# Value transposes of an HGRN2 head issued behind its diagonal products, in one place of the TensorE stream

## The chip, the cores and the metric

One core of one Trainium2 chip runs the whole program. The metric is the device time of one execution in microseconds; of several runs the median is given.

## The reference, cut to what matters

Two layers over 1024 prompt tokens and 8x4 sample tokens, width 1024, all float32. Layer 0 is a gated short convolution, layer 1 the HGRN2 recurrence with 8 heads of 128x128 state. The change touches layer 1 alone. There each head h needs four projections (q, f, i, z) of all 1056 tokens and the chunked recurrence:

```python
proj = h @ w_in
q, fpre, inp, z = jnp.split(proj, 4, axis=-1)
q = silu(q) * HEAD_DK ** -0.5 ; vv = inp
log_f = maximum(logaddexp(log(lb), log1p(-lb) + log_sigmoid(fpre)), LOG_F_FLOOR)
k = -expm1(log_f)
# per head: S_t = diag(f_t) S_{t-1} + k_t^T v_t ,  o_t = q_t S_t
o, S = hgrn2_chunked(q, k, vv, log_f, s0)
o = rms_norm(o, g_onorm) ; y = (o * silu(z)) @ w_out
```

The prompt starts from a zero state, the sample rows from `state_hgrn`, one state per batch entry.

## The kernel before, in words

**Layout.** Activations lie feature by token: the projection of one head is a tile of 128 features by 1056 tokens, computed as three groups of 352 tokens, each 24 matmuls (8 slices of the input width, three high/low products of split fp32r operands; line 565). Four projections of a head are thus 12 groups. While the projections of head j run, the recurrence of head j-1 is done in places between the groups: `iteration(j, last)` (line 887) calls `rec(j-1, s, last)` after group s, s = 0 to 11, on TensorE, on VectorE (line 1873 on) and on ScalarE (line 1277). There is no planner; the order of each engine's queue is this hand-written one, and engines meet at semaphores. `Events` objects (PR for TensorE, VR for VectorE, AR for ScalarE) number the signals of a head in the order in which they are issued, so a wait names a signal and the count follows. The last head (h = 7) has no projections beside it; there the places are filled with parts of the output projection (`first_parts`, `part`) and with idle transposes (`keep_pace`, line 928) (lines 921 to 948).

**The places that matter here.** Place s=0: nine transposes turn the output of the head before (lines 794, 795). Place s=1, TensorE: eight transposes of the values `r_vr` into banks 5 and 6, one of the three-fold stacked sample values into bank 7 (lines 809, 810), signal `vt`. ScalarE then copies bank 7 to `v_stk` (line 1296, signal `vh`) and banks 5, 6 to `r_vt` (line 1298, signal `vt`), and writes the high half of the earlier head's output (`turn_hi`, line 1273). VectorE at s=1 multiplies the keys and queries by their gates (line 1903, 2112 columns, signal `kq`), then subtracts in `v_stk` (line 1907, `vl`), copies the sample values (line 1909, `vs`), and writes the low half of the earlier head's output (`turn_lo`, line 1871). Place s=3, TensorE: after waiting for `vs`, 16 products of 64x64 on the diagonal (line 816; 32 records in the trace, since each product is recorded twice) and one of 32x32 for the samples (line 818, two records), signal `dg`. VectorE at s=3 waits for `dg`, then line 1915 (`u2`), two predicated copies (line 1918, `am`), one small one (line 1922, `as`), then twice a whole-width multiply and a small one (lines 1928, 1931, `w4`), line 1936, 1937, and at last the stacked keys into `k_stk` (line 1940, `k3c`), for which it first waits for GpSimd. Place s=5, TensorE: waits for `k3c`, transposes the stacked keys (line 822) and runs the products of level 8 (line 786).

**GpSimd** (`spread_v`, line 511): per head a memset of ones, after `kq` a memset of the score tile (line 519, signal `am_zero`), and after `vs` one multiply of 96x1024 elements that spreads the stacked sample values over the batch entries (line 521, signal `pool_rec`). It reads `v_stk`, which shares its memory with `k_stk`; hence the wait before line 1940.

**Weights.** Each projection's weights are loaded by the SP queue, split by ScalarE (line 984, high half) and VectorE (line 1426, low half, `split_lo`) into two slots, one projection ahead. In the last head the same two lines split the rows of the output weights; `first_parts(k)` waits for `split_lo` of row k.

Of the kernel before, what the change touches and what calls it, by code (L numbers as in the profile page):

```python
# [22 lines left out]
F32 = mybir.dt.float32  # L23
F32R = mybir.dt.float32r
U8 = mybir.dt.uint8
ALU = mybir.AluOpType
ACT = mybir.ActivationFunctionType
AX = mybir.AxisListType

P = 128  # L30
# [5 lines left out]
NSAMP = NB * NS  # L36
# [3 lines left out]
CK = NP // P  # L40
# [44 lines left out]
def build(nc, x_prompt, x_sample, state_conv, state_hgrn, norm_pre, w_in, conv_w, lb_logits, onorm,  # L85
          w_out, norm_post, y_prompt, y_sample, conv_p, conv_s, hgrn_p, hgrn_s):
    ctx = ExitStack()
    with ctx:
# [3 lines left out]
        def sem(name):  # L92
            return ctx.enter_context(nc.semaphore(name))
# [35 lines left out]
        ident = sb("ident", [P, P])  # L129
# [66 lines left out]
        r_vt = pl.take((CK + 1) * P)  # L196
# [9 lines left out]
        STK = 3 * NSAMP  # L206
# [26 lines left out]
        def o_part(i, half):  # L233
# [53 lines left out]
        S_SUM = Events(sem("sample_sum_dve"), ["y0", "y1"])  # L287
        V_Y = Events(sem("out2_sum"), ["y0", "y1"])
        q_sig, z_sig = sem("q_sig"), sem("z_sig")
        PR = Events(sem("rec_pe"), ["vt", "dg", "kst", "L8", "L16", "us", "os", "L32", "L64",  # L290
                                    "kt", "u", "o0", "o1"])
        VR = Events(sem("rec_dve"), ["lb", "v3", "qc", "k", "fa", "f", "tt", "g4", "g3", "ri", "i3", "i2", "i1", "kq",
                                     "vl", "vs", "u2", "am", "as", "w4", "u4", "qb", "k3c", "kl", "w8", "c8", "u8", "w16", "c16", "u16", "w32", "c32", "u32", "ss",
                                     "sn0", "snew", "w64", "c64", "u64"]
                    + [f"s{c}" for c in range(CK)] + ["r0", "r1", "rs", "on0", "on1", "ons"])
        AR = Events(sem("rec_act"), ["gc", "vh", "vt", "kts", "os", "sqs", "kt", "sq0", "sq1", "sd"])
# [233 lines left out]
        def _(pe):  # L530
# [239 lines left out]
            def tokens(c, n=P):  # L770
                return slice(c * P, c * P + n)
# [25 lines left out]
            def rec(h, s, last):  # L797

                if s == 0:
                    if last is not None:  # L800
                        turn_output(last)
                elif s == 1:
                    for c in range(NCH):
                        pe.wait_ge(bank_free[c], emptied(bank_use(NW2) + 2 + 4 * h))
                    if last is not None:
                        pe.wait_ge(o_rdy, last + 1)
                    pe.wait_ge(VR.sem, VR.at(h, "v3"))
                    for c in range(CK):
                        nc.tensor.transpose(bank[5 + c // 4][:, tokens(c % 4)], r_vr[:, tokens(c)], ident[:, :])
                    nc.tensor.transpose(bank[7][0:STK, 128:256], r_vt[:, CK * P:CK * P + STK], ident[:, :]).then_inc(PR.now("vt"), 1)  # L810
                elif s == 3:

                    pe.wait_ge(VR.sem, VR.at(h, "vs"))
                    for i in range(2 * CK):
                        at, rows = i * HP, slice(i % 2 * HP, (i % 2 + 1) * HP)
                        nc.tensor.matmul(bank[3 + i // CK][rows, i % CK * HP:(i % CK + 1) * HP], r_K[:, at:at + HP],  # L816
                                         r_Q[:, at:at + HP], start=True, stop=True)
                    nc.tensor.matmul(bank[7][0:NSAMP, 0:NSAMP], r_K[:, NP:], r_Q[:, NP:], start=True,
                                     stop=True).then_inc(PR.now("dg"), 1)
                elif s == 5:  # L820
                    pe.wait_ge(VR.sem, VR.at(h, "k3c"))
                    nc.tensor.transpose(bank[7][0:STK, 0:P], k_stk[:, 0:STK], ident[:, :]).then_inc(PR.now("kst"), 1)
# [153 lines left out]
        def _(act):  # L976
# [293 lines left out]
            def turn_hi(h):  # L1270

                act.wait_ge(o_rdy, h + 1)
                A(reg_b[:, bass.ds(h * 2 * T, T)], r_o, ACT.Copy).then_inc(o_hi, 1)
# [3 lines left out]
            def rec(h, s, last):  # L1277
# [10 lines left out]
                elif s == 1:  # L1288

                    if last is None:  # L1290
                        act.wait_ge(V_TR.sem, V_TR.at(TT - 1, "lo"))
                    else:
                        act.wait_ge(sp_out, h * 16)
                    act.dma_start(states, state_hgrn[0, :, bass.ds(h, 1)].rearrange("b h k v -> k (b h) v")).then_inc(s0_in, 16)
                    act.wait_ge(PR.sem, PR.at(h, "vt"))
                    A(v_stk[0:STK, :], bank[7][0:STK, P:2 * P], ACT.Copy).then_inc(AR.now("vh"), 1)
                    for half in range(2):
                        ins = A(r_vt[:, half * 512:(half + 1) * 512], bank[5 + half][:, :], ACT.Copy)
                    ins.then_inc(AR.now("vt"), 1)
                    if last is not None:  # L1300
                        turn_hi(last)
                elif s == 5:
                    act.wait_ge(PR.sem, PR.at(h, "kst"))
                    act.wait_ge(pool_rec, h + 1)
                    A(kv_stk[0:STK, CK * P:], bank[7][0:STK, 0:P], ACT.Copy).then_inc(AR.now("kts"), 1)
                elif s == 6:
                    act.wait_ge(PR.sem, PR.at(h, "os"))
                    A(r_os[:, :], bank[7][:, 0:P], ACT.Copy).then_inc(AR.now("os"), 1)
                    act.wait_ge(AR.sem, AR.at(h, "os"))
                    A(bank[7][:, P:2 * P], r_os[:, :], ACT.Square,  # L1310
                      accum_out=small[:, CK:CK + 1]).then_inc(AR.now("sqs"), 1)
                elif s == 7:
                    act.wait_ge(VR.sem, VR.at(h, "snew"))
                    act.dma_start(hgrn_s[0, :, bass.ds(h, 1)].rearrange("b h k v -> k (b h) v"), states).then_inc(s0_out, 16)
                elif s == 8:
                    act.wait_ge(PR.sem, PR.at(h, "kt"))
                    for half in range(2):
                        ins = A(r_kt[:, half * 512:(half + 1) * 512], bank[5 + half][:, :], ACT.Copy)
                    ins.then_inc(AR.now("kt"), 1)
                elif s == 10:  # L1320
                    act.wait_ge(PR.sem, PR.at(h, "o1"))
                    for half in range(2):
                        A(r_sq[:, half * 512:(half + 1) * 512], bank[3 + half][:, :], ACT.Square).then_inc(AR.now(f"sq{half}"), 1)
                    act.wait_ge(VR.sem, VR.at(h, "r1"))
                    A(small[:, 16:17 + CK], small[:, 0:CK + 1], ACT.Sqrt, bias=eps[:, :], scale=1.0 / P).then_inc(AR.now("sd"), 1)
                    act.wait_ge(VR.sem, VR.at(h, f"s{CK - 1}"))
                    act.dma_start(hgrn_p[0, 0, bass.ds(h, 1)].rearrange("h k v -> k (h v)"),
                                  r_s[:, (CK - 1) * P:]).then_inc(sp_out, 16)
# [90 lines left out]
        def _(dve):  # L1419
# [454 lines left out]
            def rec(h, s, last, final=False):  # L1874
# [23 lines left out]
                elif s == 1:  # L1898
# [2 lines left out]
                    dve.wait_ge(AR.sem, AR.at(h, "gc"))  # L1901
                    dve.wait_ge(pool_one, h + 1)
                    V.tensor_tensor(r_kq, r_kq, arena[:, 0:2 * T], ALU.mult).then_inc(VR.now("kq"), 1)
                    dve.wait_ge(PR.sem, PR.at(h, "vt"))
                    dve.wait_ge(AR.sem, AR.at(h, "vh"))
                    third = slice(2 * NSAMP, 3 * NSAMP)
                    V.tensor_tensor(v_stk[third, :], bank[7][third, P:2 * P], v_stk[third, :].bitcast(F32),
                                    ALU.subtract).then_inc(VR.now("vl"), 1)
                    V.tensor_copy(r_vt[0:NSAMP, CK * P:], bank[7][0:NSAMP, P:2 * P]).then_inc(VR.now("vs"), 1)
                    if last is not None and not final:  # L1910
                        turn_lo(last)
                elif s == 3:
# [4 lines left out]
                    for half in range(2):  # L1917
                        ins = V.copy_predicated(r_am[:, half * 512:(half + 1) * 512].rearrange("p (c t) -> p c t", c=4),
                                                mask8[:, :].unsqueeze(1).broadcast_to([P, 4, P]),
                                                bank[3 + half][:, :].rearrange("p (c t) -> p c t", c=4))  # L1920
                    ins.then_inc(VR.now("am"), 1)
                    V.copy_predicated(r_as[:, :], mask4[:, :], bank[7][0:NSAMP, 0:NSAMP]).then_inc(VR.now("as"), 1)
                    dve.wait_ge(VR.sem, VR.at(h, "u2"))

# [154 lines left out]
```

## Time and profile before

| | us |
|---|---|
| median of 3 runs | 1077.96 |
| lowest, highest | 1077.11, 1078.79 |
| the profiled execution, its own time | 1079.18 |
| its span, first to last instruction | 1077.5 |
| TensorE busy in the span | 1052.9 (98%) |
| VectorE busy | 724.4 (67%) |
| ScalarE busy | 384.8 (36%) |
| GpSimd busy | 38.6 (4%) |

The mean granted TensorE clock of the span is 0.995 of full speed. Seven heads (h = 0 to 6) run beside projections, about 62 us each, from about 500 to 935 us; the last head and the output projection follow. In the rows of a timeline the columns are: start and duration in us, engine, line, operation, output <- input by the program's names, partitions x elements, count of merged instructions, and in brackets the idle time just before and what ended it. DVE is VectorE, ACT ScalarE, POOL GpSimd, PE TensorE. A matmul's duration runs to its modelled end, so its successor starts before that; starts are what tells the pace.

### The profile page before, as it was taken

To read this page: it belongs to the slowest core of one execution; us is meant where nothing else is said; L and a number is where in the kernel's file an instruction comes from. 1 tells how busy PE (TensorE), PEld (TensorE's weight loads), DVE (VectorE), ACT (ScalarE), POOL (GpSimd) and SP (SyncE) were. 2 spreads that over 40 slices of the span, in tenths; PEclk is the share of its full clock that TensorE was granted. 3 is DMA by queue.
4 is the path that set the end of the run, shared out by engine and by line. 5 is a ranking of instruction groups with operands and counts; after the bars stand their busy time and mean duration, and the time that the engine had idled before them with its cause. 6 is when DMAs were issued, how large, how long until landed. Compare 5 with 4: busy or idle time off the path is not lost.

```text
span 1077.5 us, 20495 instructions
## 1 busy us (share of the span) xinstructions
PE 1052.9 (98%) x8043; PEld 987.8 (92%) x8043; DVE 724.4 (67%) x1294; ACT 384.8 (36%) x730; POOL 38.6 (4%) x53
## 2 busy tenths in 40 slices
PE   6999999999999999999999999999999999979997
PEld 5999999999999888789999999999999999967885
DVE  7798677677677645655658595775859577575146
ACT  7443333333334433443243242414233241533123
POOL 1000000000000000000101010010101010010000
PEclk9999999999999999999999999999999999989999
DMA  7102121121121352122212211211221121121143
GB/s 231 33 20 79 42 77 39 39 78 39 39 78 58 115 181 99 64 64 59 60 42 60 60 41 58 60 40 41 58 61 41 56 61 58 42 79 59 47 174 123
DMA packets 93317, 74.30 MB, mean 69 GB/s; under 512 B 2519, under 2 KB 85528, under 8 KB 93274
## 3 DMA queue, kind: packets, MB, share of 16 engines
q1 hardware_dynamic: 75482, 64.80, 19.2%
q10 hardware_dynamic: 17792, 8.91, 2.8%
q8 instruction: 29, 0.48, 0.2%
q14 instruction: 14, 0.11, 0.0%
HBM read 60.26 MB, written 13.44 MB: 68 GB/s over the span
## 4 chain that ended last, share of the span: by engine, by line
PE 89%; DVE 7%; DMA 2%; issue 1%; ACT 1%; SPq 0%; DVEq 0%; ACTq 0%
PE bank L565 34%; PE bank L613 23%; PE bank L712 17%; PE bank L585 2%; PE bank L786 2%; PE bank L859 1%; PE bank L866 1%; PE bank L780 1%; PE bank L868 1%; DMA wraw<-in_w_in 1%; PE bank L816 1%; DMA arena<-in_x_prompt 1%; PE bank L727 1%; PE bank L693 1%; PE bank L689 1%
## 5 line engine op out<-in xcount | busy, mean ns | idle before, releaser
L565 PE MATMUL bank<-reg_a,wsplit 128*128 128x352 f32 x2304 | 388.5, 326 | 0.6 <-ACT arena L1236 0.6
L565 PEld LDWEIGHTS bank<-reg_a,wsplit 128*128 128x128 f32 x2304 | 367.8, 188 | 4.0 <-issue 2.4
L613 PE MATMUL bank<-reg_a,wsplit 128*128 128x264 f32 x1344 | 165.5, 284 | 0.0
L613 PEld LDWEIGHTS bank<-reg_a,wsplit 128*128 128x128 f32 x1344 | 164.1, 188 | 0.0
L613 PE MATMUL bank<-reg_b,w_ring 128*128 128x264 f32 x1008 | 125.0, 284 | 1.0 <-ACT arena L1091 1.0
L613 PEld LDWEIGHTS bank<-reg_b,w_ring 128*128 128x128 f32 x1008 | 123.3, 188 | 1.3 <-DVE arena L1545 1.0
L712 PE MATMUL bank<-reg_a,reg_b 128*128 128x512 f32 x288 | 71.3, 402 | 0.9 <-DVE reg_a L1426 0.9
L712 PE MATMUL bank<-reg_b,reg_a 128*128 128x512 f32 x288 | 68.7, 395 | 0.0
L712 PEld LDWEIGHTS bank<-reg_a,reg_b 128*128 128x128 f32 x288 | 55.0, 192 | 14.3 <-DVE reg_a L1426 1.3
L712 PEld LDWEIGHTS bank<-reg_b,reg_a 128*128 128x128 f32 x288 | 53.9, 188 | 12.6
L1614 DVE TENSOR_TENSOR arena<-arena,bank 128x264 f32<-128x264 f32 x84 | 34.8, 427 | 33.6 <-PE bank L613 32.4
L1069 ACT ACTIVATE w_ring<-wraw 128x512 fp32r<-128x512 f32 x42 | 26.1, 631 | 68.8 <-PE bank L613 68.8
L1091 ACT ACTIVATE arena<-bank 128x264 f32<-128x264 f32 x84 | 31.9, 389 | 48.8 <-PE bank L613 44.1
L1426 DVE TENSOR_TENSOR wsplit<-wraw,wsplit 128x1024 fp32r<-128x1024 f32 x36 | 43.8, 1218 | 4.7 <-ACT wsplit L984 4.7
L1069 ACT ACTIVATE wsplit<-wraw 128x512 fp32r<-128x512 f32 x42 | 25.0, 627 | 57.4 <-DMA wraw<-in_w_in 44.1
L1811 DVE TENSOR_TENSOR arena<-arena,r_tt 128x512 f32<-128x512 f32 x32 | 22.1, 689 | 32.3 <-PE bank L786 20.1
L1236 ACT ACTIVATE arena<-bank 128x352 f32<-128x352 f32 x24 | 11.1, 462 | 90.7 <-PE bank L565 61.4
L1731 DVE TENSOR_TENSOR arena<-bank,arena 128x512 f32<-128x512 f32 x24 | 16.3, 686 | 39.3 <-ACT arena L1182 39.2
L1998 DVE SCALAR_TENSOR_TENSOR arena<-arena,bank 128x352 f32<-128x352 f32 x45 | 22.7, 516 | 21.2 <-ACT arena L1234 12.0
L1234 ACT ACTIVATE arena<-bank 128x352 f32<-128x352 f32 x21 | 9.7, 464 | 74.5 <-PE bank L565 74.5
L984 ACT ACTIVATE wsplit<-wraw 128x1024 fp32r<-128x1024 f32 x34 | 35.8, 1056 | 0.0
L517 POOL MEMSET arena<- 128x264 f32 x8 | 5.5, 688 | 831.4 <-DVE r_tt L1858 783.8
(260 smaller groups left out, 1481.9 us busy)
## 6 DMA issues: line engine op xcount, KB each, us to landing
wraw<-in_w_in SPq DMA_DIRECT2D x64, 512.0 KB, 4.0
arena<-in_x_prompt SPq DMA_DIRECT2D x16, 512.0 KB, 3.6
wraw<-in_w_out SPq DMA_DIRECT2D x16, 512.0 KB, 3.3
x_scratch<-arena SPq DMA_DIRECT2D x8, 512.0 KB, 2.6
arena<-in_state_hgrn ACTq DMA_DIRECT2D x8, 512.0 KB, 3.9
out<-arena ACTq DMA_DIRECT2D x8, 512.0 KB, 3.0
arena<-x_scratch SPq DMA_DIRECT2D x8, 512.0 KB, 3.2
out<-arena SPq DMA_DIRECT2D x7, 512.0 KB, 2.9
```

Source lines behind the costliest of these rows:

```text
L565: mm = nc.tensor.matmul(bank[b][:, 0:CH], w[wi][:, k, :], rhs[hi], start=(k == 0 and i == 0), stop=(k == KT - 1 and i == 2))
L585: mm = nc.tensor.matmul(bank[b][:, 0:QT], w[wi][:, k, :], src[hi][:, k % KH, cols], start=(k == 0 and i == 0), stop=(k == KT - 1 and i == 2))
L613: mm = nc.tensor.matmul(bank[banks[q]][:, 0:QT], w[wi][:, k, :], B_OP[name][hi][:, k, q * QT:(q + 1) * QT], start=(start and k == 0 and i ...
L712: mm = nc.tensor.matmul(bank[b][0:r, :], src[side][:, k, i * P:i * P + r], w[wi][:, half * HALF:(half + 1) * HALF], start=(start and side ...
L786: mm = nc.tensor.matmul(b[rows, i * HP // 2:(i + 1) * HP // 2].rearrange("p (b r) -> p b r", r=m), r_K[:, at:at + HP], rhs, start=True, st ...
L984: A(wsplit[:, s, 0] if dst is None else dst, wraw[:, s], ACT.Copy).then_inc(w_hi, 1)
L1069: A(w_block(name)[0], A_RAW[name], ACT.Copy).then_inc(W_HI.now(name), 1)
L1091: A(dst[:, q * QT:(q + 1) * QT], bank[banks[q]][:, 0:QT], ACT.Copy).then_inc(C_ACT.now(f"{what}{s}{q}"), 1)
L1426: V.tensor_tensor(d, wraw[:, s], h.bitcast(F32), ALU.subtract).then_inc(w_lo, 1)
L1614: V.tensor_tensor(dst[:, cols], src[:, cols], bank[banks[q]][:, 0:QT], ALU.add).then_inc(C_DVE.now(f"{what}{s}{q}"), 1)
L1811: V.tensor_tensor(qr, qr, tl.unsqueeze(2).broadcast_to([P, nb, m]), ALU.mult)
L1998: V.scalar_tensor_tensor(buf[:, cols], buf[:, cols], QSCALE if kind == "q" else 1.0, bank[c][:, 0:CH], ALU.mult, ALU.mult).then_inc(bank_f ...
```

## The change

At TensorE place s=1 no longer does anything. Place s=3 now holds, in this order: the waits that s=1 had (the three banks emptied, the earlier output read), a wait for `kq` in place of `vs`, the transpose of the stacked sample values, the diagonal products (signal `dg`), and the eight transposes of the values (signal `vt`). ScalarE's two copies move from s=1 to s=3, the first released by `dg`, the second by `vt`; VectorE's lines 1907 and 1909 move from between `kq` and `turn_lo` to between `am` and `as`. The lists of signals are reordered to match.

```diff
--- before.py
+++ after.py
@@ -287,10 +287,10 @@
         S_SUM = Events(sem("sample_sum_dve"), ["y0", "y1"])
         V_Y = Events(sem("out2_sum"), ["y0", "y1"])
         q_sig, z_sig = sem("q_sig"), sem("z_sig")
-        PR = Events(sem("rec_pe"), ["vt", "dg", "kst", "L8", "L16", "us", "os", "L32", "L64",
+        PR = Events(sem("rec_pe"), ["dg", "vt", "kst", "L8", "L16", "us", "os", "L32", "L64",
                                     "kt", "u", "o0", "o1"])
         VR = Events(sem("rec_dve"), ["lb", "v3", "qc", "k", "fa", "f", "tt", "g4", "g3", "ri", "i3", "i2", "i1", "kq",
-                                     "vl", "vs", "u2", "am", "as", "w4", "u4", "qb", "k3c", "kl", "w8", "c8", "u8", "w16", "c16", "u16", "w32", "c32", "u32", "ss",
+                                     "u2", "am", "vl", "vs", "as", "w4", "u4", "qb", "k3c", "kl", "w8", "c8", "u8", "w16", "c16", "u16", "w32", "c32", "u32", "ss",
                                      "sn0", "snew", "w64", "c64", "u64"]
                     + [f"s{c}" for c in range(CK)] + ["r0", "r1", "rs", "on0", "on1", "ons"])
         AR = Events(sem("rec_act"), ["gc", "vh", "vt", "kts", "os", "sqs", "kt", "sq0", "sq1", "sd"])
@@ -799,24 +799,23 @@
                 if s == 0:
                     if last is not None:
                         turn_output(last)
-                elif s == 1:
+                elif s == 3:
+
                     for c in range(NCH):
                         pe.wait_ge(bank_free[c], emptied(bank_use(NW2) + 2 + 4 * h))
                     if last is not None:
                         pe.wait_ge(o_rdy, last + 1)
-                    pe.wait_ge(VR.sem, VR.at(h, "v3"))
-                    for c in range(CK):
-                        nc.tensor.transpose(bank[5 + c // 4][:, tokens(c % 4)], r_vr[:, tokens(c)], ident[:, :])
-                    nc.tensor.transpose(bank[7][0:STK, 128:256], r_vt[:, CK * P:CK * P + STK], ident[:, :]).then_inc(PR.now("vt"), 1)
-                elif s == 3:
-
-                    pe.wait_ge(VR.sem, VR.at(h, "vs"))
+                    pe.wait_ge(VR.sem, VR.at(h, "kq"))
+                    nc.tensor.transpose(bank[7][0:STK, 128:256], r_vt[:, CK * P:CK * P + STK], ident[:, :])
                     for i in range(2 * CK):
                         at, rows = i * HP, slice(i % 2 * HP, (i % 2 + 1) * HP)
                         nc.tensor.matmul(bank[3 + i // CK][rows, i % CK * HP:(i % CK + 1) * HP], r_K[:, at:at + HP],
                                          r_Q[:, at:at + HP], start=True, stop=True)
                     nc.tensor.matmul(bank[7][0:NSAMP, 0:NSAMP], r_K[:, NP:], r_Q[:, NP:], start=True,
                                      stop=True).then_inc(PR.now("dg"), 1)
+                    for c in range(CK):
+                        mm = nc.tensor.transpose(bank[5 + c // 4][:, tokens(c % 4)], r_vr[:, tokens(c)], ident[:, :])
+                    mm.then_inc(PR.now("vt"), 1)
                 elif s == 5:
                     pe.wait_ge(VR.sem, VR.at(h, "k3c"))
                     nc.tensor.transpose(bank[7][0:STK, 0:P], k_stk[:, 0:STK], ident[:, :]).then_inc(PR.now("kst"), 1)
@@ -1292,13 +1291,15 @@
                     else:
                         act.wait_ge(sp_out, h * 16)
                     act.dma_start(states, state_hgrn[0, :, bass.ds(h, 1)].rearrange("b h k v -> k (b h) v")).then_inc(s0_in, 16)
+                    if last is not None:
+                        turn_hi(last)
+                elif s == 3:
+                    act.wait_ge(PR.sem, PR.at(h, "dg"))
+                    A(v_stk[0:STK, :], bank[7][0:STK, P:2 * P], ACT.Copy).then_inc(AR.now("vh"), 1)
                     act.wait_ge(PR.sem, PR.at(h, "vt"))
-                    A(v_stk[0:STK, :], bank[7][0:STK, P:2 * P], ACT.Copy).then_inc(AR.now("vh"), 1)
                     for half in range(2):
                         ins = A(r_vt[:, half * 512:(half + 1) * 512], bank[5 + half][:, :], ACT.Copy)
                     ins.then_inc(AR.now("vt"), 1)
-                    if last is not None:
-                        turn_hi(last)
                 elif s == 5:
                     act.wait_ge(PR.sem, PR.at(h, "kst"))
                     act.wait_ge(pool_rec, h + 1)
@@ -1901,12 +1902,6 @@
                     dve.wait_ge(AR.sem, AR.at(h, "gc"))
                     dve.wait_ge(pool_one, h + 1)
                     V.tensor_tensor(r_kq, r_kq, arena[:, 0:2 * T], ALU.mult).then_inc(VR.now("kq"), 1)
-                    dve.wait_ge(PR.sem, PR.at(h, "vt"))
-                    dve.wait_ge(AR.sem, AR.at(h, "vh"))
-                    third = slice(2 * NSAMP, 3 * NSAMP)
-                    V.tensor_tensor(v_stk[third, :], bank[7][third, P:2 * P], v_stk[third, :].bitcast(F32),
-                                    ALU.subtract).then_inc(VR.now("vl"), 1)
-                    V.tensor_copy(r_vt[0:NSAMP, CK * P:], bank[7][0:NSAMP, P:2 * P]).then_inc(VR.now("vs"), 1)
                     if last is not None and not final:
                         turn_lo(last)
                 elif s == 3:
@@ -1919,6 +1914,11 @@
                                                 mask8[:, :].unsqueeze(1).broadcast_to([P, 4, P]),
                                                 bank[3 + half][:, :].rearrange("p (c t) -> p c t", c=4))
                     ins.then_inc(VR.now("am"), 1)
+                    dve.wait_ge(AR.sem, AR.at(h, "vh"))
+                    third = slice(2 * NSAMP, 3 * NSAMP)
+                    V.tensor_tensor(v_stk[third, :], bank[7][third, P:2 * P], v_stk[third, :].bitcast(F32),
+                                    ALU.subtract).then_inc(VR.now("vl"), 1)
+                    V.tensor_copy(r_vt[0:NSAMP, CK * P:], bank[7][0:NSAMP, P:2 * P]).then_inc(VR.now("vs"), 1)
                     V.copy_predicated(r_as[:, :], mask4[:, :], bank[7][0:NSAMP, 0:NSAMP]).then_inc(VR.now("as"), 1)
                     dve.wait_ge(VR.sem, VR.at(h, "u2"))
 
```

## Rows read from the trace of the kernel before

**Rows 1.** The page: the engines' busy time, the chain that ended last.
```profile
PE 1052.9 (98%) x8043; PEld 987.8 (92%) x8043; DVE 724.4 (67%) x1294; ACT 384.8 (36%) x730; POOL 38.6 (4%) x53
...
PE 89%; DVE 7%; DMA 2%; issue 1%; ACT 1%; SPq 0%; DVEq 0%; ACTq 0%
```

**Rows 2.** Timeline of TensorE around place s=1 of head 3; the last row up to 700 us.
```profile
692.55 1.04 PE L809 MATMUL bank<-ident,arena 128*128 128x128 f32 x8
693.42 0.27 PE L810 MATMUL bank<-ident,arena 128*96 128x128 f32 x1
...
693.70 6.57 PE L565 MATMUL bank<-reg_a,wsplit 128*128 128x352 f32 x40
```

**Rows 3.** Timeline of TensorE around place s=3 of head 3.
```profile
701.06 0.32 PE L565 MATMUL bank<-reg_a,wsplit 128*128 128x352 f32 x1
...
701.31 1.15 PE L816 MATMUL bank<-arena 128*64 128x64 f32 x32
...
702.57 0.59 PE L565 MATMUL bank<-reg_a,wsplit 128*128 128x352 f32 x2
```

**Rows 4.** Timeline of TensorE at place s=5 of head 3.
```profile
710.37 0.27 PE L822 MATMUL bank<-ident,r_os 128*96 128x128 f32 x1
710.57 1.12 PE L786 MATMUL bank<-arena 128*64 128x32 f32 x32
```

**Rows 5.** Timeline of TensorE in the last head: the first transpose after level 32.
```profile
969.62 0.33 PE L928 MATMUL bank<-ident 128*128 128x128 f32 x1
```

**Rows 6.** Timeline of VectorE in head 3.
```profile
697.29 2.34 DVE L1903 TENSOR_TENSOR arena<-arena 128x2112 f32<-128x2112 f32 x1
...
700.29 1.26 DVE L1871 TENSOR_TENSOR reg_b<-arena,reg_b 128x1056 f32 x1
...
702.68 0.92 DVE L1915 TENSOR_TENSOR r_tt<-r_tt 128x264 f32<-128x264 f32 x1 [0.24 <-PE bank L818]
...
704.85 1.21 DVE L1928 TENSOR_TENSOR arena<-arena,r_tt 128x1024 f32<-128x1024 f32 x1
...
707.95 1.22 DVE L1426 TENSOR_TENSOR wsplit<-wraw,wsplit 128x1024 fp32r<-128x1024 f32 x1
```

**Rows 7.** Timelines: GpSimd's multiply in heads 0, 3 and 7; VectorE's line 1915 in heads 0 and 7.
```profile
514.32 1.90 POOL L521 TENSOR_TENSOR kv_stacked<-v_stacked,bmask 96x1024 fp32r<-96x1024 f32 x1
...
516.92 0.43 DVE L1915 TENSOR_TENSOR r_tt<-r_tt 128x264 f32<-128x264 f32 x1 [0.24 <-PE bank L818]
...
700.61 2.70 POOL L521 TENSOR_TENSOR kv_stacked<-v_stacked,bmask 96x1024 fp32r<-96x1024 f32 x1
...
946.70 2.66 POOL L521 TENSOR_TENSOR kv_stacked<-v_stacked,bmask 96x1024 fp32r<-96x1024 f32 x1
...
947.77 1.88 DVE L1915 TENSOR_TENSOR r_tt<-r_tt 128x264 f32<-128x264 f32 x1 [0.17 <-PE bank L818]
```

**Rows 8.** Timeline of ScalarE in head 3.
```profile
693.91 1.07 ACT L1298 ACTIVATE arena<-bank 128x512 f32<-128x512 f32 x2
...
706.73 0.47 ACT L1234 ACTIVATE arena<-bank 128x352 f32<-128x352 f32 x1 [4.85 <-PE bank L565]
```

**Rows 9.** Timeline of the last head, VectorE and TensorE.
```profile
943.36 2.36 DVE L1903 TENSOR_TENSOR arena<-arena 128x2112 f32<-128x2112 f32 x1
...
946.40 1.15 PE L816 MATMUL bank<-arena 128*64 128x64 f32 x32 [1.18 <-DVE arena L1909]
...
949.87 1.04 PE L928 MATMUL bank<-ident 128*128 128x128 f32 x8
...
955.26 4.21 PE L712 MATMUL bank<-wsplit,reg_b 128*128 128x512 f32 x9 [4.36 <-DVE wsplit L1426]
...
961.33 2.35 PE L712 MATMUL bank<-reg_a,reg_b 128*128 128x512 f32 x9
```

**Rows 10.** Table by stretch of the last head: us; PE, PEld, DVE, ACT, POOL busy; granted clock; DMA share; GB/s.
```profile
951.00:954.27 3.27, 0.00 (x0) 0.00 (x0) 3.23 (x8) 1.04 (x1) 0.00 (x0) 1.00 0.00 0
...
955.26:961.10 5.84, 5.84 (x38) 4.49 (x40) 1.36 (x2) 1.07 (x2) 0.00 (x0) 0.50 0.55 182
```

## The prediction

> **What bounds the kernel now.** The page comes first: TensorE is busy 98% of the span and carries 89% of the chain that ended last, VectorE only 7% [rows 1]. So in the stretch from about 500 to 935 us, where a head's recurrence lies between the projections of the next, work or waits off TensorE cost nothing until they make it late. The second view is TensorE's timeline in one such head: its groups of matmuls follow one another without an idle stretch, at 0.16 us a matmul ((6.57 - 0.33) / 39) [rows 2]. The third view is the last head, which has no projections to hide behind. There TensorE waits 1.18 us for line 1909 before the diagonal products, and 4.36 us for line 1426, which stands in VectorE's queue behind the whole of its place s=3 [rows 9]. So the change has two accounts: seven heads in which only TensorE's own time counts, and one in which VectorE's queue does.
>
> The profiled execution took 1079.18 us, 1.7 more than its span and 1.2 more than the median. The changes below are made against that execution and then put on the median. A difference of 0.2%, 2.2 us, is about what a measurement of this kernel can tell from no change.
>
> **The place taken away on TensorE.** Does a place cost anything beside its own instructions? At s=1 the rows say no: the first transpose starts at 692.55, the projection is back at its pace at 693.70, which without the place would have been 692.55 + 0.16. The place cost 0.99 us, and its nine transposes at 0.11 each are 0.98 ((693.42 - 692.55) / 8) [rows 2]. Nothing is left for the switch, and the transposes stay. Place s=3 does pay for switching: from 701.06 to the second projection matmul after it, 702.57 + 0.26, less two paces, is 1.45 us, of which the products are about 1.1 [rows 3].
>
> The new place, from rows of the same kinds: the stacked transpose follows a projection without loss and the products follow it after 0.20, as line 786 follows line 822 [rows 4]; the products to the small one's end, 702.57 - 701.31 = 1.26 with the 0.12 of the switch in it [rows 3]; then eight transposes. The first transpose behind level 32 in the last head shows how that switch goes: it lasts 0.33 where another lasts 0.27 [rows 5, 2], 0.06 more. So 0.06 + 7 x 0.11 = 0.83 to the eighth's start and, as after s=1, 0.28 less one pace to the projection's pace, 0.12. Sum 0.20 + 1.26 + 0.83 + 0.12 = 2.41 against 0.99 + 1.45 = 2.44. The small gap ahead of the products also shrinks by about 0.03. That makes 0.03 to 0.08 us a head; I take 0.06, seven times: **-0.4 us**. Bounds: nothing, or 0.1 a head, -0.7.
>
> The Trainium skill (TensorEngine Tiling (Array Packing), Key Properties) says that a change of tiling mode drains TensorE. The new order has as many changes of mode as the old, so by that rule, too, the removed place gives nothing back.
>
> **Waits of the seven heads.** The products now wait for `kq`, the end of line 1903 at 699.63, and TensorE reaches them 0.98 earlier, at 700.33, since s=1 is empty: 0.7 us of cover [rows 6, 3]. VectorE loses lines 1907 and 1909 here (from 699.63 to 700.29, 0.66 us), so `turn_lo` and the two evacuations behind it move up; none of them is late. ScalarE's copies come behind the products: about 1.4 us ending near 704, while it is idle until 706.73 less 0.98 [rows 8]. Cost nothing. No DMA is issued in the moved lines; SP's queue sees only a release of weight slots that shifts by under 1.5 us, with a whole projection of cover.
>
> **VectorE's place s=3, and GpSimd.** This is the term that can hurt. GpSimd's multiply of line 521 is released by `vs`. It takes 1.90 us in head 0, where VectorE ran beside it nothing with both inputs in SBUF [rows 7]. In head 3 it takes 2.70: line 1871 held VectorE until 701.55, and 701.55 + 1.76 is where the multiply ends, 703.31. Line 1915, started at 702.68, ends 0.29 after that, at 703.60, in 0.92 where it takes 0.43 alone [rows 6, 7]. In the last head it starts at 947.77 and ends 0.29 after the multiply, in 1.88 us. Of the eight heads only the first shows no hold; in the other seven the 0.29 is the same. So the two engines shut each other out, an instruction at a time. Now `vs` comes behind `am`, and the next thing VectorE does that reads SBUF twice is line 1928. It gets the multiply's 1.9 us in its way, less 0.14 of its own start that overlaps and less the small line 1922: about 1.7. If line 1928 wins instead, the multiply is late and line 1940 waits for it: the same sum.
>
> The Trainium skill (SBUF — State Buffer, Who interferes with whom) says that a VectorE instruction with two SBUF inputs contends with a GpSimd one that reads SBUF, and that the loser blocks fully. That speaks against this change, since line 1928 is of that form; by it alone the stall is certain, the trace shows it only for line 1915 and, the other way about, for the multiply.
>
> New chain in a middle head: the products start 0.98 - 0.20 earlier, so `dg` reaches VectorE at 702.68 - 0.78 = 701.90; line 1915 alone 0.43; `am` and `as` 1.25 (703.60 to 704.85); lines 1907 and 1909 0.66; lines 1928 to 1940 3.10 (704.85 to 707.95); stall 1.7. That is 709.0 for `k3c`, before 707.95 [rows 6]. TensorE asks for it at 710.37 less 0.06 [rows 4]: 1.3 us of cover are left of 2.4. Line 1426 then ends at 710.2, TensorE needs its weights at 711.6. **Cost nothing**, by a margin that is no longer large. The bounds of the stall: 0, or 2.7, the whole of the longest row; both still fit.
>
> **The last head.** TensorE no longer waits for line 1909 but for line 1903, which ends at 945.72: the products start at 945.76 + 0.20 instead of 946.40, `dg` comes 0.44 earlier [rows 9]. VectorE then needed 1.88 + 1.25 + 3.09 = 6.22 to line 1426 (953.99); now 0.43 + 1.25 + 0.66 + 3.09 + 1.7 = 7.13. Net 7.13 - 6.22 - 0.44 = **+0.5 us**, straight on the path, since TensorE waits for that line 1426 [rows 9] and its own chain runs on from there. Bounds: with no stall on line 1928, 5.43 - 6.22 - 0.44 = -1.2; with 2.7, +1.5. I take 1.7 because rows 7 show the hold in seven heads of eight. The transposes behind the products end near 948.2, ScalarE's 1.4 us of copies near 949.6 [rows 8]; `keep_pace`, which waits for them now, stood at 949.87 and moves to about 950.3 [rows 9].
>
> The wait of 4.36 us also lowers the clock: the granted clock is 1.0 to 954.27, TensorE having done nothing since 951, and 0.5, the 1.2 GHz level, to 961.10 [rows 10]. Nine matmuls there take 4.21 us, the same nine later 2.35 [rows 9]; with the places between, the low clock costs some 2.5 us. The new idle stretch is about 4.5 us, so I keep this cost. It can fall differently from run to run, by up to that 2.5.
>
> **Sum.** -0.4 + 0.5 = +0.1 us: 1079.3 for the profiled execution, 1078.1 on the median; a hundredth of a per cent, so no change. Chance 0.78.
>
> **Rival, faster (0.13).** Line 1928 is not shut out, or the multiply runs wholly beside lines that don't mind it. Then the last head gives -1.2, and its idle stretch shrinks from 4.4 to 2.7 us, so that the clock may not fall: -2.5 more. With -0.4 that is -1.6 to -4.1: 1073.9 to 1076.4. For it: only line 1915 has been seen waiting. Against: it waits to the same 0.29 each time, and line 1928 has the same two inputs in SBUF.
>
> **Rival, slower (0.09).** TensorE waits for `k3c` at place s=5 of the middle heads. The point from which it decides is 1.3 us beyond my 709.0. It would need VectorE shut out twice, once by the multiply for line 1928 and again for a later line, some 3.3 us in all. Then each head pays the excess; 0.5 us a head is 3.5 in seven, plus 2 in the last head: 1083. For it: cover halves. Against: the multiply is one instruction of 1.9 us, and VectorE and GpSimd one behind the other wholly are already in my sum.
>
> That the change does nothing at all is inside the first case.
>
> **How the numbers follow.** The forecast is 1078.1. Its own range is +-1.9 (the clock's 2.5 cut at either end, the stall's bounds). Reaching into the faster case: 1075.9 to 1080.0. Faster by over 0.2%: 0.13; within: 0.78; slower: 0.09.
>
> **What the changed profile would show.** No transposes of line 809's kind between the second and third group of a head, and the place of the products some 2.4 us long, with no idle time before line 822. Line 1915 at 0.43 us in every head. Line 1928's first instance 2.9 instead of 1.2 us, or the multiply longer than 3 us. In the last head `dg` about 0.4 earlier and line 1426, with TensorE behind it, about 0.5 later against the products of the head before. An idle stretch ahead of line 822 in the middle heads, a first line 1928 of 1.2 us beside a multiply of 1.9, or a last head without the half clock would prove me wrong.

## The result, and the profile after

The changed kernel takes 1081.88 us, median of 7 runs (1080.05 to 1083.33), the kernel before 1077.11 beside it (7 runs, 1076.38 to 1079.38): ratio 1.004, interval 1.0028 to 1.0052. It is slower by 4.8 us in the medians (3.0 to 5.6 by the interval), where no change was forecast, and outside the range. The profiled execution took 1081.48 us, its span is 1079.8.

The page of the changed kernel, the lines that answer to [rows 1]:

```profile
PE 1051.5 (97%) x8043; PEld 985.0 (91%) x8043; DVE 734.0 (68%) x1294; ACT 386.5 (36%) x730; POOL 42.4 (4%) x53
...
PE 80%; DVE 11%; issue 3%; ACT 3%; DMA 2%; ACTq 0%; SPq 0%; DVEq 0%
```

TensorE does the same work in the same busy time, but the chain that ended last has moved off it: 80% where it was 89%, VectorE 11% where it was 7%. Something in the middle heads now waits for VectorE. The view of one line, L565 of the changed kernel, says what:

```profile
its engine sat idle before it (us, times) until:
  issue: 7.6, 14
  DVE wsplit L1427: 3.7, 7
  ACT arena L1235: 0.6, 1
```

Seven times, once a head, the projections wait for the VectorE half of the weight split (line 1427, line 1426 before): 0.2 us in head 0, 0.56 to 0.62 us in each of heads 1 to 6. The kernel before has no such entry. Its `issue` entry is 2.4, 8; the 5.2 us more here are the same six stops, seen from the weight loads of TensorE, which sat idle 0.85 to 0.91 us at each. The timelines of head 3, TensorE first:

```profile
688.48 1.03 PE L794 MATMUL bank<-ident,arena 128*128 128x128 f32 x8
...
689.38 7.94 PE L565 MATMUL bank<-reg_a,wsplit 128*128 128x352 f32 x48
697.88 4.11 PE L565 MATMUL bank<-reg_a,wsplit 128*128 128x352 f32 x24 [0.57 <-DVE wsplit L1427]
701.83 0.27 PE L809 MATMUL bank<-ident,arena 128*96 128x128 f32 x1
702.03 1.15 PE L812 MATMUL bank<-arena 128*64 128x64 f32 x32
703.12 0.25 PE L814 MATMUL bank<-arena 128*32 128x32 f32 x2
703.29 1.09 PE L817 MATMUL bank<-ident,arena 128*128 128x128 f32 x8
704.14 7.93 PE L565 MATMUL bank<-reg_a,wsplit 128*128 128x352 f32 x48
711.91 0.27 PE L821 MATMUL bank<-ident,r_os 128*96 128x128 f32 x1
...
751.17 1.03 PE L794 MATMUL bank<-ident,arena 128*128 128x128 f32 x8
```

VectorE and GpSimd in the same head:

```profile
696.54 1.21 DVE L1427 TENSOR_TENSOR wsplit<-wraw,wsplit 128x1024 fp32r<-128x1024 f32 x1
...
703.40 0.43 DVE L1910 TENSOR_TENSOR r_tt<-r_tt 128x264 f32<-128x264 f32 x1 [0.35 <-PE bank L814]
...
705.87 1.21 DVE L1928 TENSOR_TENSOR arena<-arena,r_tt 128x1024 f32<-128x1024 f32 x1
707.00 1.86 DVE L1931 TENSOR_TENSOR arena<-arena,r_tt 128x16 f32<-128x16 f32 x1
...
705.81 3.02 POOL L521 TENSOR_TENSOR kv_stacked<-v_stacked,bmask 96x1024 fp32r<-96x1024 f32 x1 [4.34 <-DVE arena L1921]
```

The head lasts 751.17 - 688.48 = 62.69 us (the six intervals between heads 1 and 7 are 62.70 to 62.76). Here are the rows of the kernel before that the prediction did not read, its two place s=0 starts, its third and fourth group, and its split:

```profile
687.71 1.03 PE L794 MATMUL bank<-ident,arena 128*128 128x128 f32 x8
...
693.45 7.93 PE L565 MATMUL bank<-reg_a,wsplit 128*128 128x352 f32 x48
...
749.63 1.03 PE L794 MATMUL bank<-ident,arena 128*128 128x128 f32 x8
...
695.73 1.20 DVE L1426 TENSOR_TENSOR wsplit<-wraw,wsplit 128x1024 fp32r<-128x1024 f32 x1
```

A head took 61.92 us. Its 48 matmuls from 693.45 are two groups; the second of them, the fourth of the head, belongs to the next projection and starts at 693.45 + 3.93 = 697.38. Its weights were ready at 695.73 + 1.20 = 696.93. That is a cover of 0.45 us (the time by which awaited work is done before it is asked for), and the nine transposes at s=1, 0.98 us, stood ahead of it. With them gone, TensorE is at the fourth group at 689.38 + 48 x 0.164 = 697.2 of the changed trace, 0.5 us before the split ends at 696.54 + 1.21 = 697.75.

The last head, TensorE:

```profile
949.69 0.28 PE L809 MATMUL bank<-ident,arena 128*96 128x128 f32 x1 [1.56 <-DVE arena L1904]
949.90 1.15 PE L812 MATMUL bank<-arena 128*64 128x64 f32 x32
...
959.80 3.64 PE L712 MATMUL bank<-wsplit,reg_b 128*128 128x512 f32 x9 [4.58 <-DVE wsplit L1427]
```

**Where the time went.** All kernels of this study can be cut at the same starts on TensorE: the first matmul of line 565, place s=0 of heads 1 and 7, the products of head 7, the restart behind the long wait (the first matmul with the second part of the output weights), the turn of the last output, the end. Stretches in us, from one profiled execution each:

| | start | to head 1 | heads 1 to 7 | to products | to restart | to last turn | to end |
|---|---|---|---|---|---|---|---|
| before | 461.94 | 101.93 | 371.52 | 11.01 | 8.86 | 57.84 | 64.35 |
| changed | 460.94 | 102.05 | 376.30 | 10.61 | 9.90 | 55.61 | 64.35 |
| difference | -1.00 | +0.12 | +4.78 | -0.40 | +1.04 | -2.23 | 0.00 |

The first column lies ahead of everything the change touches and varies between 460.9 and 462.4 in the traces of this study. The sixth column, from the restart to the turn of the last output, holds the half clock. In the profiled execution before it came twice: from 954.27 to 961.10, which the prediction read, and again from 978.18 to 981.59, which it did not. In this one it came once, for 3.4 us: ```profile
960.51:963.92 3.41, 3.41 (x15) 2.25 (x15) 0.37 (x1) 0.23 (x1) 0.00 (x0) 0.50 0.77 231
```

What belongs to the change is 0.12 + 4.78 - 0.40 + 1.04 = +5.5 us, of which the middle heads are nearly all.

## Experiments

Two theories stood after this reading. **W**: the empty place s=1 brings TensorE to weights that aren't split yet. **P**: the heads are longer because GpSimd's multiply now shuts VectorE out inside its place s=3.

**The split moved forward.**

```diff
+                        if c == 0 and t == 0:
+                            split_lo(4 * j + (NW2 + t + 1), t % 2)
                         rec(j - 1, 3 * t + c, last)
-                        if c == 0:
+                        if c == 0 and t:
                             split_lo(4 * j + (NW2 + t + 1), t % 2)
```

> The changed kernel, with one VectorE instruction per head moved forward: the low half of the weight split for the fourth group of a head (line 1427) stands ahead of the output gate of place s=0 instead of behind it. Theory W (with place s=1 empty, TensorE comes to the fourth group 0.98 us earlier and finds its weights not yet split; the row has 0.57 us idle, the pace loses about 0.83): the idle time before L565 that VectorE's split ended is gone, a middle head takes 61.87 us (61.92 before, 62.71 changed), and the whole is 5 to 6 us faster than the changed kernel, within 1 us of the kernel before. Theory P (the heads are longer because GpSimd's multiply shuts VectorE out for 1.7 us at place s=3): a head stays at 62.7 us and the whole stays 4 to 5 us above the kernel before.

1077.35 us against 1077.12 (ratio 1.0003, 0.9994 to 1.0011): the loss is gone. TensorE in head 3, and VectorE's split there:

```profile
687.23 1.04 PE L794 MATMUL bank<-ident,arena 128*128 128x128 f32 x8
...
688.13 11.78 PE L565 MATMUL bank<-reg_a,wsplit 128*128 128x352 f32 x72
699.75 0.27 PE L809 MATMUL bank<-ident,arena 128*96 128x128 f32 x1
...
749.09 1.04 PE L794 MATMUL bank<-ident,arena 128*128 128x128 f32 x8
...
688.82 1.22 DVE L1427 TENSOR_TENSOR wsplit<-wraw,wsplit 128x1024 fp32r<-128x1024 f32 x1
```

Three groups in one row without a gap, the split 6.5 us earlier against place s=0, 61.86 us a head. P falls: VectorE's place s=3 was left as the change has it, and GpSimd's multiply still takes 3.02 us and the small line 1931 1.86. The gain in the median is 4.5 us, somewhat under the 5 to 6 expected; the traces give it as 5.1 in heads 1 to 7.

**The value transposes alone.** The kernel before with the eight transposes of the values and their ScalarE copies moved; the sample transpose, lines 1907, 1909 and the multiply stay. The part on TensorE:

```diff
-                    for c in range(CK):
-                        nc.tensor.transpose(bank[5 + c // 4][:, tokens(c % 4)], r_vr[:, tokens(c)], ident[:, :])
-                    nc.tensor.transpose(bank[7][0:STK, 128:256], r_vt[:, CK * P:CK * P + STK], ident[:, :]).then_inc(PR.now("vt"), 1)
+                    nc.tensor.transpose(bank[7][0:STK, 128:256], r_vt[:, CK * P:CK * P + STK], ident[:, :]).then_inc(PR.now("vst"), 1)
...
                                      stop=True).then_inc(PR.now("dg"), 1)
+                    for c in range(CK):
+                        mm = nc.tensor.transpose(bank[5 + c // 4][:, tokens(c % 4)], r_vr[:, tokens(c)], ident[:, :])
+                    mm.then_inc(PR.now("vt"), 1)
```

> The kernel before, with only the eight value transposes and ScalarE's copies of them moved behind the diagonal products; the stacked sample transpose, lines 1907 and 1909 and so GpSimd's multiply stay at s=1. Theory W: s=1 is shorter by 0.87 us, the cover of the fourth group's weights was 0.45, so TensorE waits there and a head takes 62.6 to 62.8 us; GpSimd's multiply stays at 2.70 us with line 1915 at 0.9 to 1.0. Over the kernel before: 7 x 0.75 = 5 us slower less what the last head gives. Theory P: nothing is moved on VectorE or GpSimd, so a head stays at 61.9 us and the time at that of the kernel before.

1080.48 us (1.0034, 1.0021 to 1.0048), 62.6 us a head. The view of line 565:

```profile
  issue: 6.9, 14
  DVE wsplit L1429: 2.7, 6
```

The loss appears with the multiply in its old place, so eight transposes leaving s=1 are enough for it. It is 3.4 us between the medians where I expected 5 less the last head's gain; in the heads it is 375.61 - 371.52 = 4.1.

**Idle transposes in the gap.**

```diff
+                elif s == 1:
+                    if last is not None:
+                        pe.wait_ge(o_rdy, last + 1)
+                    for k in range(5):
+                        nc.tensor.transpose(bank[7][:, 384:512], ident[:, :], ident[:, :])
                 elif s == 3:
```

> The changed kernel with five idle transposes of the identity (0.55 us) put into the empty place s=1 of each head. Theory W: they lie in the wait for the weights; the idle time before the fourth group falls from 0.57 to about 0, and a head stays at 62.7 us (62.65 to 62.75), the whole within 1 us of the changed kernel. Rival S (the changed place s=3 itself, its switches of tile form and its waits, is what costs 0.79 us a head): the five add their 0.55 us to each head, 63.25 us, and 4 us to the whole.

```profile
694.61 0.71 PE L806 MATMUL bank<-ident 128*128 128x128 f32 x5
695.08 8.25 PE L565 MATMUL bank<-reg_a,wsplit 128*128 128x352 f32 x48
```

1082.83 us (1.005, 1.0033 to 1.0066), and 62.7 us a head (376.42 for the six against 376.30): 0.55 us of work a head went in for next to nothing, since it took the place of idle time. Head 0, which had only 0.2 us of it, did get 0.4 us longer. The place s=3 of the changed kernel is not what costs.

**The multiply beside instructions that read PSUM.** In the changed kernel, VectorE's order u2, am, vl, vs, as becomes u2, vl, vs, am, as.

```diff
+                    dve.wait_ge(AR.sem, AR.at(h, "vh"))
+                    third = slice(2 * NSAMP, 3 * NSAMP)
+                    V.tensor_tensor(v_stk[third, :], bank[7][third, P:2 * P], v_stk[third, :].bitcast(F32),
+                                    ALU.subtract).then_inc(VR.now("vl"), 1)
+                    V.tensor_copy(r_vt[0:NSAMP, CK * P:], bank[7][0:NSAMP, P:2 * P]).then_inc(VR.now("vs"), 1)
                     for half in range(2):
...
                     ins.then_inc(VR.now("am"), 1)
-                    dve.wait_ge(AR.sem, AR.at(h, "vh"))
...
-                    V.tensor_copy(r_vt[0:NSAMP, CK * P:], bank[7][0:NSAMP, P:2 * P]).then_inc(VR.now("vs"), 1)
```

> The changed kernel, with VectorE's place s=3 reordered: the two sample instructions stand right behind u2 and ahead of the two predicated copies (which read PSUM), so that GpSimd's multiply runs beside those. Theory W with my term for the last head: a middle head stays at 62.7 us; the small line 1931 or line 1928 is no longer held for 1.7 us but for 0.3 to 0.6; in the last head the wait of TensorE for the split ends 1.1 to 1.4 us earlier after its start, which is what the whole gains, more if the clock doesn't fall. Theory P: the heads, too, come down by 0.5 us or more each, the whole by 4 us or more.

The last head:

```profile
953.94 1.89 POOL L521 TENSOR_TENSOR kv_stacked<-v_stacked,bmask 96x1024 fp32r<-96x1024 f32 x1 [1.86 <-DVE arena L1916]
...
953.89 1.38 DVE L1918 COPY_PREDICATED arena<-mask_within,bank 128x512 f32<-128x512 uint8 x2
955.26 1.66 DVE L1928 TENSOR_TENSOR arena<-arena,r_tt 128x1024 f32<-128x1024 f32 x1
```

The multiply lasts its 1.9 us beside two predicated copies that lose nothing (1.38), and line 1928 is held for 0.45 instead of line 1931 for 1.7. Products to restart: 8.65 us, before 8.86, changed 9.90. The heads stay at 62.7, as W wants. The whole did not show the gain: 1082.07 us (1.0042, 1.0027 to 1.0056), where 1.3 less than the changed kernel was expected; the four runs spread over 2.4 us and can't resolve that. The gain is shown in the stretch, and in the next kernel.

**Both edits**, the split forward and the multiply beside the copies, in the changed kernel:

> The changed kernel with both edits: the split of the fourth group's weights moved forward and the sample instructions ahead of the predicated copies. Theory W and the shut-out taken as separate terms: a middle head 61.86 us as with the split alone, the last head from its products to TensorE's restart 8.65 us as with the reorder alone (8.86 before, 9.90 changed). Against the kernel before: -0.36 in the heads, -0.41 to the products, -0.2 to the restart, 1.0 us faster at equal clock, ratio 0.999. Rival (the two edits share their gain): restart still 9 us or more, no gain over the kernel before.

1075.10 us against 1078.06 (0.9977, 0.9966 to 0.9987). Heads 1 to 7 take 371.16 us, the products 10.65, the restart 8.65: the terms add as expected, to -0.9 us. The measured gain is 2.5 us by the ratio and 3.0 between the medians, more than that. The rest is the clock; TensorE around the restart:

```profile
954.14 2.37 PE L712 MATMUL bank<-wsplit,reg_b 128*128 128x512 f32 x9 [3.31 <-DVE wsplit L1427]
```

The nine matmuls take 2.37 us instead of 4.21 [rows 9]: with an idle stretch of 3.3 us instead of 4.4, the granted clock stayed at 2.4 GHz in this execution. None of the 35 runs of the kernel before, beside these, shows a mean clock above 0.998, and 23 show 0.994 or 0.995; of the 11 of this kernel 3 show 1.0 and one 0.994. Runs with the same mean clock can be compared without that term. At 0.996 to 0.998, twelve runs of the kernel before average 1076.67 us and seven of this one 1075.61: 1.1 us less, close to the 1.0 expected at equal clock.

**Line 1915 behind the copies**, in the kernel before:

```diff
-                    V.tensor_tensor(every(r_tt[:, :], 2, 0), every(r_tt[:, :], 2, 0), every(r_tt[:, :], 2, 1),
-                                    ALU.mult).then_inc(VR.now("u2"), 1)
+                    V.memset(small[:, 46:47], 0.0)
                     for half in range(2):
...
                     V.copy_predicated(r_as[:, :], mask4[:, :], bank[7][0:NSAMP, 0:NSAMP]).then_inc(VR.now("as"), 1)
+                    V.tensor_tensor(every(r_tt[:, :], 2, 0), every(r_tt[:, :], 2, 0), every(r_tt[:, :], 2, 1),
+                                    ALU.mult).then_inc(VR.now("u2"), 1)
```

> The kernel before, with VectorE's line 1915 (u2, two inputs in SBUF) put behind the predicated copies, which read PSUM, so that GpSimd's multiply has ended when it comes; one memset of a single column takes over the wait. Theory (the engines shut each other out only where VectorE reads SBUF twice): line 1915 lasts 0.43 to 0.6 us in every head instead of 0.92 to 1.88, the last head's restart comes 7.6 to 7.8 us after its products instead of 8.86, and the middle heads stay at 61.92 us. The whole 1.1 us faster at equal clock, within what a measurement can tell. Rival (line 1915 is held by something else about its place, such as the first instruction behind dg): the predicated copies stretch instead and the restart stays at 8.8.

```profile
947.01 2.67 POOL L521 TENSOR_TENSOR kv_stacked<-v_stacked,bmask 96x1024 fp32r<-96x1024 f32 x1
...
949.44 0.52 DVE L1922 TENSOR_TENSOR r_tt<-r_tt 128x264 f32<-128x264 f32 x1
...
954.38 4.21 PE L712 MATMUL bank<-wsplit,reg_b 128*128 128x512 f32 x9 [3.17 <-DVE wsplit L1426]
```

1075.63 us (0.9979, 0.9970 to 0.9987). The line takes 0.52 us here where it took 1.88 [rows 7], the restart comes 7.66 us after the products instead of 8.86, the heads stay at 61.92. The predicated copies, now first beside the multiply, did not stretch (a memset of one column stands ahead of them). So line 1915 was held because it met the multiply, not by its place behind the products. At a mean clock of 0.996 to 0.998 nine runs average 1075.53 us, 1.1 less than the kernel before, as expected; the rest of the 2.4 us between the medians is the clock.

**The early split in the kernel before** is the control:

> The kernel before, with the split of the fourth group's weights moved forward and nothing else. Theory W: its cover was 0.45 us and no wait is there to remove, so a middle head stays at 61.92 us and the time is that of the kernel before. Rival (the early split is worth something by itself, and the gain of the first run says nothing about the change): heads under 61.85 us.

1078.05 us against 1078.06 (1.0002, 0.9993 to 1.0012), every stretch to the restart the same to 0.01 us. Where the cover holds, moving the split is worth nothing.

**All three**: values behind the products, split forward, line 1915 last.

> The kernel before, with the value transposes alone moved behind the products, the split moved forward and line 1915 put last. Theory W: a middle head 61.8 to 61.9 us (the wait of 0.57 to 0.7 us that the moved transposes alone gave is gone), the last head's products at 10.9 to 11.0 us after its place s=0 and its restart 7.6 to 7.8 us after them. The whole 1.3 to 1.6 us faster than the kernel before at equal clock; the idle stretch is 2.3 us instead of 4.4, so the half clock may not come: then 2 us more. Rival: the stretch is still long enough and the clock falls as often as before.

```profile
945.11 1.15 PE L814 MATMUL bank<-arena 128*64 128x64 f32 x32 [1.95 <-DVE arena L1912]
...
946.38 1.97 PE L819 MATMUL bank<-ident,arena 128*128 128x128 f32 x8
948.00 3.15 PE L712 MATMUL bank<-wsplit,reg_b 128*128 128x512 f32 x9
...
952.80 2.36 PE L712 MATMUL bank<-wsplit,reg_b 128*128 128x512 f32 x9 [0.78 <-DVE wsplit L1429]
```

1074.89 us (0.9974, 0.9964 to 0.9983), the fastest here, though not told apart from the two others at 0.998. 61.87 us a head, restart 7.69 us after the products. The idle stretch did not come out at 2.3 us in this execution: the granted clock was 0.5 from 946.38 to 949.79, beginning 1.3 us after the end of the 1.95 us wait ahead of the products. The eight transposes took 1.97 us instead of 1.09 and the first nine matmuls 3.15 instead of 2.35, and only 0.78 us of idle time was left. At a mean clock of 0.996 to 0.998 eight runs average 1075.12 us, 1.55 less than the kernel before, within the 1.3 to 1.6 expected.

### The profile page after: what moved, and what is told of

The parts are those of the page before. It is cut to its first block, busy times and chain, and to the rows that moved or that the text cites. A ratio compares the mean times of both kernels' runs of the same rounds, so it can differ in the third digit from the quotient of the medians.

```text
span 1079.8 us, 20487 instructions
## 1 busy us (share of the span) xinstructions
PE 1051.5 (97%) x8043; PEld 985.0 (91%) x8043; DVE 734.0 (68%) x1294; ACT 386.5 (36%) x730; POOL 42.4 (4%) x53
## 4 chain that ended last, share of the span: by engine, by line
PE 80%; DVE 11%; issue 3%; ACT 3%; DMA 2%; ACTq 0%; SPq 0%; DVEq 0%
PE bank L565 26%; PE bank L613 23%; PE bank L712 16%; PE bank L585 2%; PE bank L786 2%; DMA wraw<-in_w_in 1%; PE bank L858 1%; PE bank L865 1%; PE bank L780 1%; PE bank L867 1%; DVE arena L1865 1%; PE bank L812 1%; DVE wsplit L1427 1%; DMA arena<-in_x_prompt 1%; PE bank L727 1%
## 5 line engine op out<-in xcount | busy, mean ns | idle before, releaser
L565 PE MATMUL bank<-reg_a,wsplit 128*128 128x352 f32 x2304 | 388.2, 326 | 4.1 <-DVE wsplit L1427 3.5
L565 PEld LDWEIGHTS bank<-reg_a,wsplit 128*128 128x128 f32 x2304 | 367.8, 188 | 9.1 <-issue 7.6
L712 PE MATMUL bank<-reg_a,reg_b 128*128 128x512 f32 x288 | 70.0, 396 | 1.0 <-DVE reg_a L1427 0.9
L712 PE MATMUL bank<-reg_b,reg_a 128*128 128x512 f32 x288 | 68.7, 396 | 0.0
L712 PEld LDWEIGHTS bank<-reg_a,reg_b 128*128 128x128 f32 x288 | 53.8, 188 | 14.3 <-DVE reg_a L1427 1.9
L712 PEld LDWEIGHTS bank<-reg_b,reg_a 128*128 128x128 f32 x288 | 53.9, 188 | 12.6
L1427 DVE TENSOR_TENSOR wsplit<-wraw,wsplit 128x1024 fp32r<-128x1024 f32 x36 | 43.9, 1218 | 4.7 <-ACT wsplit L983 4.7
L1235 ACT ACTIVATE arena<-bank 128x352 f32<-128x352 f32 x24 | 11.1, 463 | 90.7 <-PE bank L565 61.4
L1970 DVE COPY arena<-bank 128x128 f32<-128x128 f32 x8 | 2.3, 291 | 47.4 <-PE bank L858 47.4
```

Of the source, the lines that this page charges most:

```text
L565: mm = nc.tensor.matmul(bank[b][:, 0:CH], w[wi][:, k, :], rhs[hi], start=(k == 0 and i == 0), stop=(k == KT - 1 and i == 2))
L712: mm = nc.tensor.matmul(bank[b][0:r, :], src[side][:, k, i * P:i * P + r], w[wi][:, half * HALF:(half + 1) * HALF], start=(start and side ...
L1427: V.tensor_tensor(d, wraw[:, s], h.bitcast(F32), ALU.subtract).then_inc(w_lo, 1)
```

## Why the prediction was wrong

**The step that failed** is "Waits of the seven heads". It said that TensorE reaches the products 0.98 us earlier with 0.7 us of cover, that none of VectorE's moved instructions is late, and closed with "Cost nothing". With the weights in time that holds: in the kernel with the split forward TensorE comes to place s=3 12.52 us after place s=0, where it was 13.51 before. In the changed kernel it comes at 13.35. What the step left out is what TensorE meets on its way there: the fourth group, whose weights VectorE splits at place s=0. The split for the seventh to ninth group was looked up (its end and the 711.6 at which it is needed), and the SP queue's loads were given "a whole projection of cover"; the split ahead of the fourth group was not, though its row stands in the same timeline. Cover 0.45 against 0.98 gives a wait of about 0.5; measured are 0.57 idle by the row and 62.71 - 61.86 = 0.85 a head. It is more than the row, since the row counts idle time from a matmul's modelled end: by starts, the fourth group begins 0.73 us behind the pace (697.88 where 697.16 was due), of which 0.13 lie between the end of the split and that start. Its second matmul then follows after 0.26 us instead of 0.16. This was also no rival: the slower one had TensorE waiting in the middle heads, but for `k3c` at s=5, where there is no wait in the changed trace.

**The place taken away**: forecast 2.41 us for the new place against 0.99 + 1.45, -0.06 a head. The new place measures 2.39, and with the weights in time the head is 61.86, -0.06. Right. A place between projections costs its instructions and its switches, and the switches moved along.

**VectorE beside GpSimd**: forecast that line 1915 would be 0.43 us, and the first line 1928 2.9 or the multiply over 3. Line 1910, as it is now, is 0.43; line 1928 won, the multiply is 3.02, and the small line 1931 behind it is 1.86 instead of 0.16, held for the 1.7 of the forecast. Right in size, on another line: it was not line 1940 that waited for the late multiply, but the small line right behind line 1928. The cover before s=5 held; in the changed trace `k3c` is done at 710.74 and TensorE asks for it at 711.91. The rule of the Trainium skill (SBUF — State Buffer, Who interferes with whom), that two SBUF inputs on VectorE and a reading GpSimd instruction exclude each other, was borne out where it could be turned: the copies from PSUM passed beside the multiply (1.38 us for two), and line 1915, moved out of its way, took 0.52 us instead of 1.88.

**The last head**: forecast products 0.44 earlier and the restart 0.5 later. Measured -0.40 and, from s=0 to the restart, 20.51 against 19.87, +0.64. Right, to 0.2 us. I kept the half clock as a cost that may come or not; it came shorter in this profile and hid 2.2 us of the loss. For the fall that I had read, 2.5 us was about right. But the execution before holds a second one, and needs 57.84 us from the restart to the turn where the one without any needs 54.08: the chance in the faster rival was 3.8 us, not 2.5.

The sum was +0.1 and is +5.5 in the stretches that the change touches. The missing term is the wait for the weights: 0.85 us in each of six heads and 0.2 in head 0, 5.3 in all.

## What to carry to other kernels

Work that sits between two groups on the bounding engine also gives time to whoever prepares the next group. Before it is taken away or moved back, list every semaphore that the engine meets between the old and the new position, each with its cover, and not only those at the two ends. And if a cover is too small, the producer can often be put forward in its own queue for nothing, as here, where one instruction's place decided 5 us. In the kernel before, the same move was worth nothing, because the cover held.

## What the runs showed of the hardware

GpSimd's multiply and a VectorE instruction with two SBUF inputs exclude each other, an instruction at a time. Where the VectorE one was held, it ended later than the multiply by its own length less 0.12 to 0.14 us (line 1915: 0.29 of 0.43; line 1931: 0.03 of 0.16; line 1928 beside the moved multiply: 1.09 of 1.21). Back to back VectorE instructions of that form let the multiply in between them: in every head of the changed kernel the row of the multiply begins 0.05 or 0.06 us ahead of line 1928, line 1928 runs first in its 1.21 us, and the multiply takes its turn before line 1931, which follows without a gap.

The granted clock fell to its 1.2 GHz level in the five traces in which the wait for the output weights was 4.4 us or more; of the four with 3.2 to 3.5 us it fell in three and stayed up in one, the execution with a span of 1072.6 us. The low clock also came once, for 3.4 us, behind a wait of only 1.95 us and 1.3 us of small products. From the restart to the turn of the last output the kernels take 57.8 us in executions with 10.2 us of it in that stretch, 55.4 to 55.7 with 3.4, and 54.1 to 54.2 with none. So a wait that is 1 us shorter can save up to 3.8 us more, or nothing more, from run to run. That makes medians of this kernel uncertain by about as much as the last head's terms, and stretches between the same two instructions of two traces, which agreed to some 0.05 us where nothing between them had changed, the better measure.
